# Half of neighbourhood attention's output projection, worked in halves inside latent attention

## Chip, cores, metric

One core of one Trainium2 chip. The metric is device microseconds (us) of one execution of the whole program. Before the change three runs took 2887.43, 2887.59 and 2888.29 us; the median is 2887.59 us.

## What is computed

The reference is one step of a two-layer trunk on 128 context tokens and 512 latent tokens of width 1024, 640 in all. Only the mixer of the first layer matters here. It runs two kinds of attention on the same input, 8 heads each, and projects both outputs together:

```python
def _even_mixer_latent(h, k_ctx, v_ctx, ckv_ctx, kr_ctx, w_in, q_norm, kv_norm, w_uq, w_ukv, rpb, w_out):
    qa, ka, va, qb, ckv, kr = _even_project(h, w_in, q_norm, kv_norm, w_uq)
    oa = _neighbourhood_attention(qa, ka, va, k_ctx, v_ctx, rpb)
    ...
    kb_lat, vb_lat = _mla_keys(ckv, _axial_rope(kr), w_ukv)
    kb_ctx, vb_ctx = _mla_keys(ckv_ctx, kr_ctx[:, :, None, :], w_ukv)
    ...
    ob = _blocked_attention(qb, kb, vb, (MLA_NOPE_DIM + MLA_ROPE_DIM) ** -0.5)
    return jnp.concatenate([oa.reshape(B, L, NA_WIDTH), ob.reshape(B, L, MLA_OUT)], axis=-1) @ w_out

xs = xs + ms[:, :, 5] * ys
```

The context tokens go through the same mixer, with plain attention among their own 128 keys. Since `w_out` is linear, the kernel adds the part of the neighbourhood heads to `x` first and the part of the latent heads later.

## The kernel before

Activations lie with channels on partitions and 640 tokens as columns. Weights arrive in blocks of 1024 columns: SP loads a block into one of 4 `raw` buffers, ScalarE (ACT) rounds it to the high part, VectorE (DVE) subtracts to get the low part; these two are the `split` of a block (L915 on ACT, L1541 on DVE), and the results lie in a ring of 4 `w2` slots. A slot is free when TensorE (PE) has used the block four before it (`wt_free`, the function `done`). A product is three matmuls (high x high, high x low, low x high) for each 128 channels and each half of the tokens, 320 columns at a time.

The mixer runs in this order on PE, in the engine's own program; blocks are counted from `n0`:

1. Neighbourhood attention (units of one head and 128 queries). Its output stays in `g2`.
2. `out_proj` (L2875, called on L2942): 8 output tiles of 128 channels from `g2`, two in each of the blocks `n0+18` to `n0+21`; a tile is 4 channel groups x 3 products x 2 halves = 24 matmuls. DVE adds each tile to `x` (`add_by_rows`, L1677 and L1679).
3. Block `n0+22`: values for latent attention (`tok_tiles`, L2714), copied to `va` by ACT. Blocks `n0+23` to `n0+26`: queries and keys (`ch_tile`, L2400), copied to `qb` and `kb` by ACT (L1348, L1357), rotated on DVE.
4. `latent_attention` (L2832): 32 units, 8 for each pair of heads. In unit `l` PE issues the scores of unit `l+2` (L2729, L2730), in some units the values of a pair of earlier units (L2807), and the 5 transposes of unit `l` (L2764). Around it DVE takes the maximum (L2122), ACT the exponential (L1255), DVE divides by the sum (L2129, L2130), and ACT copies the transposed weights to `pt` (L1264). The context tokens of a pair of heads run beside this: scores in unit 2 of 8 (L2772), transposes in unit 5, values in unit 7, in bank 7 of PSUM.
5. `last_out_proj`: 8 output tiles from the latent heads' output, which ACT and DVE have put in `g2` over the neighbourhood output; then norm and FFN.

The scores of unit `l+2` wait until the exponential of unit `l` has been taken, since there are two score buffers:

```python
            def score_mm(g):
                h, b = UNITS[g]
                pe.wait_ge(s_exp, g - 1)
```

Of the kernel before, what the change touches and what calls it, by code (L numbers as in the profile page):

```python
# [71 lines left out]
EM_PAIR = [0, 1, 3, 2, 0] + [(e - 4) % 3 for e in range(5, 14)]  # L72
V_BANK = [2, 3, 4, 5, 7]
# [177 lines left out]
def build(nc, a):  # L251
# [3 lines left out]
    with ctx:  # L255
# [140 lines left out]
        va = place("va", 6 * NLAT, at=h_at + (3 * 2 * T + 4 * (PAST + T)) * 4).rearrange("p (t c) -> p t c", t=6)  # L396
        pt_ctx = place("pt_ctx", 2 * P, at=h_at + (3 * 2 * T + 4 * (PAST + T) + 6 * NLAT) * 4)
# [94 lines left out]
        cx_mm, cx_neg, cx_exp, cx_p = sem("cx_mm"), sem("cx_neg"), sem("cx_exp"), sem("cx_p")  # L492
        cx_t, cx_ev, cx_pv, cx_low = sem("cx_t"), sem("cx_ev"), sem("cx_pv"), sem("cx_low")
# [140 lines left out]
        def pt_cols(g):  # L634

            return slice(g % 4 * P, (g % 4 + 1) * P)

# [270 lines left out]
        def _(act):  # L908
# [349 lines left out]
            def pt_evac(g, na):  # L1258
                h, b = UNITS[g]
                act.wait_ge(t_mm, g + 1)  # L1260
                if g >= 4:
                    act.wait_ge(pv_mm, NU if NU <= g < NU + 4 else g - 3)
                n = 1 if b == 0 else 3 if na else 5
                act.activation(pt[:, 0:n, pt_cols(g)],  # L1264
                               turned(g)[:, 0:n * P].rearrange("p (k q) -> p k q", k=n), ACT.Copy).then_inc(t_ev, 1)

            def ctx_exp(p):
                act.wait_ge(cx_neg, p + 1)
                if p:
                    act.wait_ge(cx_t, p)  # L1270
                for v in range(2):
                    c = 4 + 2 * (p % 2) + v
                    ins = act.activation(sb3[:, v * P:(v + 1) * P], ps[:, 7, (1 + v) * P:(2 + v) * P], ACT.Exp,
# [3 lines left out]
            def ctx_evac(p):  # L1277
                act.wait_ge(cx_t, p + 1)
                if p:
                    act.wait_ge(cx_pv, p)  # L1280
                act.activation(pt_ctx, ps[:, 7, P:3 * P], ACT.Copy).then_inc(cx_ev, 1)

            def o_lat(p, cols=slice(0, NLAT), src=ps[:, 6, :]):
                act.activation(lat_of(g2[:, p, 0, :])[:, cols], src[:, cols], ACT.Copy).then_inc(o_hi, 1)
# [41 lines left out]
            for m in range(4):  # L1326
                split(n0 + 18 + m + LEAD, (n0 + 18 + m + LEAD) % RING)
# [7 lines left out]
            split(n0 + 22 + LEAD, (n0 + 22 + LEAD) % RING)  # L1335
            for t in range(6):
                if t < 5:
                    act.wait_ge(vb_mm, t + 1)
                else:
                    act.wait_ge(wt_free, done(n0 + 22))  # L1340
                act.activation(va[:, t, :], ps[:, 2 + t, :], ACT.Copy).then_inc(vb_ev, 1)

            for p in range(4):
                n = n0 + 23 + p
                split(n + LEAD, (n + LEAD) % RING)
# [7 lines left out]
                for hh in range(2):  # L1353
                    if p == 3 and hh:
# [4 lines left out]
                                   ).then_inc(mk_ev, 1)  # L1359
            for l in range(2, NL):  # L1360
# [4 lines left out]
                if i == 3:  # L1365
                    ctx_exp(p)
                if i == 6:
                    ctx_evac(p)
                if i == 0:
                    if p == 1:  # L1370
                        act.wait_ge(wt_free, done(n0 + 21))
                    act.wait_ge(cx_pv, p)
                    o_ctx(p - 1)
                if i == 1:
                    act.wait_ge(pv_mm, NU + l - 1)
                    o_lat(p - 1)
            act.wait_ge(cx_pv, 4)
            o_ctx(3)
            act.wait_ge(pv_mm, NU + NL - 2)
            o_lat(3, slice(0, 3 * P))  # L1380
            pt_evac(NU + NL - 1, False)
            act.wait_ge(pv_mm, NU + NL)
            o_lat(3, slice(3 * P, NLAT), last_out)
            for j in range(4):
                n = n0 + 27 + j
                if j < 3:
                    split(n + LEAD, (n + LEAD) % RING)
# [139 lines left out]
        def _(dve):  # L1527
# [451 lines left out]
            def last_projection(nn, n0, out_at, g, xb, l, s):  # L1979

                norm_scale(l, s)
                for j in range(4):
                    n = out_at + j
                    if j < 3:
                        split(n + LEAD)
# [147 lines left out]
            def ctx_scores(p):  # L2133
                dve.wait_ge(cx_mm, p + 1)
                dve.tensor_reduce(negmax[:, cx_cols(p)], ps[:, 7, P:3 * P].rearrange("p (v k) -> p v k", v=2), AX.X,
                                  ALU.max, negate=True).then_inc(cx_neg, 1)

            def ctx_normalise(p):
# [3 lines left out]
                both = sb3[:, 0:2 * P].rearrange("p (v k) -> p v k", v=2)  # L2142
# [3 lines left out]
            def o_lat(p, cols=slice(0, NLAT), src=ps[:, 6, :]):  # L2146
                return dve.tensor_tensor(lat_of(g2[:, p, 1, :])[:, cols], src[:, cols],
                                         lat_of(g2[:, p, 0, :])[:, cols].bitcast(fp32), ALU.subtract)

            def o_ctx(p):  # L2150
                return dve.tensor_tensor(ctx_of(g2[:, p, 1, :]), ps[:, 7, 0:P],
                                         ctx_of(g2[:, p, 0, :]).bitcast(fp32), ALU.subtract)

# [36 lines left out]
            for j in range(4):  # L2190
# [4 lines left out]
            split(n0 + 22 + LEAD)  # L2195
# [8 lines left out]
            for p in range(4):  # L2204
                split(n0 + 23 + p + LEAD)
# [13 lines left out]
            for l in range(NL):  # L2219
                p, i = divmod(l, 8)  # L2220
                if 1 < l + 1 < NL:
                    scores(NU + l + 1, False)
                normalise(NU + l)
                if i == 2:
                    ctx_scores(p)
                if i == 4:
                    ctx_normalise(p)
                if i == 0 and p:
                    dve.wait_ge(o_hi, 8 + 2 * p - 1)
                    o_ctx(p - 1).then_inc(cx_low, 1)  # L2230
                if i == 1 and p:
                    dve.wait_ge(o_hi, 8 + 2 * p)
                    o_lat(p - 1).then_inc(o_lo, 1)
            dve.wait_ge(o_hi, 15)
            o_ctx(3)
            dve.wait_ge(o_hi, 16)
            o_lat(3, slice(0, 3 * P))
            dve.wait_ge(o_hi, 17)
            o_lat(3, slice(3 * P, NLAT), last_out).then_inc(o_lo, 1)
# [146 lines left out]
        def _(pe):  # L2386
# [366 lines left out]
            def weight_mm(g, na):  # L2753

                h, b = UNITS[g]
                pe.wait_ge(s_p, g + 1)
                if na and g >= 2:
                    pe.wait_ge(t_ev, g - 1)
                elif not na:
                    pe.wait_ge(t_ev, g - 1 if g >= NU + NL - 2 else g)  # L2760
# [580 lines left out]
```

## Time and profile before

| | us |
|---|---|
| median of the runs | 2887.59 |
| span of the profiled execution, first to last instruction | 2885.2 |
| median less that span | 2.4 |
| PE busy in the span | 2841.8 (98%) |
| DVE busy | 2112.8 (73%) |
| ACT busy | 1190.9 (41%) |
| output projection of neighbourhood attention and maps of latent attention (672.54 to 742.10 us from the span's start) | 69.56 |
| units of latent attention (742.10 to 822.57) | 80.47 |

The page of the profile gives one span and no own time for the profiled execution apart from it; what lies around the span is the 2.4 us between it and the median. "Busy" on PE counts from the first to the modelled end of each matmul, so a busy share says that matmuls follow each other closely, not that the array is full. The granted TensorE clock is 1.00 in both stretches, the higher of its two levels.

### The profile page before, as it was taken

Reading aid. Unit: us, or ns where it says so; the run is one execution under the profiler, and the core shown is the slowest. Engines: PE = TensorE matmul, PEld = TensorE weight load, DVE = VectorE, ACT = ScalarE, POOL = GpSimd, SP = SyncE. Lnnn points to the kernel's source line nnn. Section 1 sums busy time; section 2 is a strip of 40 time slices with the busy share of each in tenths; the row PEclk is TensorE's granted clock in tenths of the full one; section 3 lists DMA queues with packets and bytes.
Section 4 is the critical chain, followed back from the end, with each engine's and each line's share of the span. In section 5 each row is a group of like instructions: output and inputs, shape, how many; then the busy total and the mean of one; then the engine's idle time right before and its main releaser. Section 6 shows DMA issues by size and latency. Waiting matters only on the chain. (4 is left out here: it accounts for less than half of the span.)

```text
span 2885.2 us, 46747 instructions
## 1 busy us (share of the span) xinstructions
PE 2841.8 (98%) x18154; PEld 2658.3 (92%) x18154; DVE 2112.8 (73%) x4053; ACT 1190.9 (41%) x2212; POOL 347.7 (12%) x436
## 2 busy tenths in 40 slices
PE   8999999999999999999999999999999999999998
PEld 5999999978789999999999998798887988999998
DVE  5898987766768989778878775755747467866856
ACT  5433535254666334356334354223233144533433
POOL 1000003120031000021000022202112033000001
PEclk9999999999999999999999999999999999999999
DMA  7544343521014433424433222324223231422221
GB/s 258 147 150 132 107 127 119 180 74 47 23 46 131 152 119 105 130 79 116 130 100 103 92 96 94 111 94 125 68 87 116 81 132 37 105 78 88 76 86 66
DMA packets 94238, 303.52 MB, mean 105 GB/s; under 512 B 10753, under 2 KB 21281, under 8 KB 93121
## 3 DMA queue, kind: packets, MB, share of 16 engines
q1 hardware_dynamic: 67328, 223.03, 23.8%
q0 software_dynamic: 21296, 63.58, 8.0%
q10 hardware_dynamic: 5392, 13.92, 1.3%
q8 instruction: 144, 2.36, 0.3%
q14 instruction: 78, 0.63, 0.1%
HBM read 285.14 MB, written 7.49 MB: 101 GB/s over the span
## 5 line engine op out<-in xcount | busy, mean ns | idle before, releaser
L2566 PE MATMUL ps<-g,w 128*128 128x320 f32 x4224 | 624.8, 308 | 0.0
L2566 PEld LDWEIGHTS ps<-g,w 128*128 128x128 f32 x4224 | 620.6, 187 | 0.8
L2533 PE MATMUL ps<-h,w 128*128 128x320 f32 x3744 | 578.3, 309 | 8.4 <-ACT swu L1022 4.6
L2533 PEld LDWEIGHTS ps<-h,w 128*128 128x128 f32 x3744 | 556.0, 188 | 10.3 <-ACT swu L1022 5.7
L2533 PE MATMUL ps<-e,w 128*128 128x320 f32 x2808 | 437.3, 309 | 0.1
L2533 PEld LDWEIGHTS ps<-e,w 128*128 128x128 f32 x2808 | 418.2, 188 | 0.4 <-DMA e<-tsum 0.4
L1541 DVE TENSOR_TENSOR w<-raw,w 128x1024 fp32r<-128x1024 f32 (+1 forms) x243 | 277.5, 1146 | 160.9 <-ACT w L915 144.7
L2714 PE MATMUL ps<-w,h 128*128 128x512 f32 x1596 | 367.4, 391 | 0.1
L2714 PEld LDWEIGHTS ps<-w,h 128*128 128x128 f32 x1596 | 298.1, 188 | 62.7 <-ACT rg L1486 1.0
L928 ACT ACTIVATE w<-w2s 128x512 fp32r<-128x512 f32 x312 | 194.1, 631 | 275.2 <-DVE w2s L1693 84.2
L915 ACT ACTIVATE w<-raw 128x1024 fp32r<-128x1024 f32 x123 | 128.9, 1061 | 264.2 <-PE ps L2400 130.9
L1720 DVE TENSOR_TENSOR w<-w2s,w 128x512 fp32r<-128x512 f32 x312 | 209.6, 684 | 3.6 <-ACT w L928 2.4
L2400 PE MATMUL ps<-h,w 128*128 128x320 f32 (+1 forms) x1344 | 204.2, 312 | 0.0
L2400 PEld LDWEIGHTS ps<-h,w 128*128 128x128 f32 x1344 | 199.0, 188 | 1.7 <-issue 1.4
L1670 DVE SCALAR_TENSOR_TENSOR x<-ps,gate,x 128x128 f32<-128x128 f32 x216 | 108.3, 545 | 125.7 <-PE ps L2566 113.2
L922 ACT ACTIVATE w<-raw 128x768 fp32r<-128x768 f32 (+1 forms) x120 | 106.0, 886 | 220.9 <-PE ps L2566 189.0
L933 ACT ACTIVATE w<-raw 128x512 fp32r<-128x512 f32 x234 | 145.0, 624 | 70.4 <-PE ps L2566 70.1
L781 POOL DMA_DIRECT2D cond<-in_ada x80 | 43.0, 538 | 920.8 <-DVE acol L1556 914.9
L733 POOL TENSOR_TENSOR tmp_q<-tmp_q 128x320 f32<-128x320 f32 (+1 forms) x72 | 79.1, 1099 | 594.9 <-ACT tmp_q L962 585.9
L2400 PE MATMUL ps<-g,w 128*128 128x320 f32 x888 | 131.4, 309 | 0.0
L2400 PEld LDWEIGHTS ps<-g,w 128*128 128x128 f32 x888 | 130.4, 188 | 0.3 <-issue 0.3
L1556 DVE CUSTOM_DVE_ANT_0 unused<-cond,crow 128x512 f32<-128x512 f32 x160 | 110.1, 688 | 9.8 <-DMA cond<-in_ada 5.3
(305 smaller groups left out, 3672.4 us busy)
## 6 DMA issues: line engine op xcount, KB each, us to landing
raw<-in_ws SPq DMA_DIRECT2D x303, 512.0 KB, 3.7
cond<-in_ada POOLq DMA_DIRECT2D x80, 512.0 KB, 3.9
raw<-in_ws SPq DMA_DIRECT2D x96, 384.0 KB, 3.1
raw<-in_ada SPq DMA_DIRECT2D x32, 512.0 KB, 3.6
cond_em<-in_ada POOLq DMA_DIRECT2D x16, 512.0 KB, 3.9
e<-tsum POOLq DMA_DIRECT2D x12, 640.0 KB, 6.3
ada<-in_ada SPq DMA_DIRECT2D x5, 1024.0 KB, 17.9
rst<-in_state ACTq DMA_DIRECT2D x4, 1024.0 KB, 4.8
```

Of the source, the lines that this page charges most:

```text
L915: act.activation(w2[:, slot_of(n), 0, :], raw_of("w", n), ACT.Copy).then_inc(wt_hi, 1)
L922: act.activation(w2[:, slot_of(n), 0, 0:cols], raw_of("w", n)[:, 0:cols], ACT.Copy).then_inc(wt_hi, 1)
L928: act.activation(left(q, f, m, 0), left_value(q, f, m), ACT.Copy).then_inc(left_hi, 1)
L933: act.activation(left(q, f, m, 0), quarter(b, half), ACT.Copy).then_inc(left_hi if m == 0 else wt_hi, 1)
L1541: dve.tensor_tensor(w2[:, slot, 1, 0:cols], raw_of("w", n)[:, 0:cols], w2[:, slot, 0, 0:cols].bitcast(fp32), ALU.subtract).then_inc(wt_lo, 1)
L1556: dve.tensor_tensor_reduce(at if row else spare, at, rows[:, row, c0:c1], 1.0, 0.0, ALU.mult, ALU.add, acol[:, k, to:to + 1]).then_inc(ada ...
L1670: ins = dve.scalar_tensor_tensor(part(xn[:, m, :]), part(pair(pr)), g[:, m, st:st + 1], part(xn[:, m, :]), ALU.mult, ALU.add)
L1720: dve.tensor_tensor(lo, left_value(q, f, m) if m else quarter(n, 0), hi, ALU.subtract).then_inc(left_lo, 1)
L2400: mm = pe.matmul(pair_half(pr, half, width), w2[:, slot, wi, at:at + cols], rhs(k, ri)[:, half * width:(half + 1) * width], start=(k == 0 ...
L2533: mm = pe.matmul(ps[:, 4 * s + bank, 0:HT], w2[:, at // 2, wi, c:c + P], rhs(k, ri), start=start and k + wi + ri == 0, stop=(k == 3 and wi ...
L2566: mm = pe.matmul(pair_half(pr, half), w2[:, slot_of(n), wi, c:c + P], half_of(g2[:, k, ri, :], half), start=k + wi + ri == 0, stop=(k == n ...
L2714: mm = pe.matmul(ps[:, bank_of(t), :], ones_tile(src(k, ri), t), w2[:, slot_of(n), wi, kk * 512:(kk + 1) * 512], start=(k == 0 and ri == 0 ...
```

## The change

Four of the eight output tiles of neighbourhood attention (tiles 4 to 7) leave step 2. They are worked in halves inside latent attention: a half tile is 12 matmuls, three to a unit (six in unit 1, none in unit 0), all into bank 7 of PSUM, and DVE adds each half to `x` after its fourth group. The blocks of these tiles move behind the maps in the stream of weights (`n0+25` and `n0+26`; the values' block becomes `n0+20`), so the splits of the blocks after them come at other places: `n0+24` before the maps, one at the end of each of the four rounds of maps, and `n0+29` in unit 17. The context tokens' work in latent attention moves from bank 7 into the free columns of the transposes' bank 5 and to other units: scores in unit 0 of 8, transposes in unit 4, values in unit 5; ACT first copies the scores to `sbc` and takes the exponential from there. Since `g2` is still read, the latent heads' output goes to `m2`, which lies over `h2`.

The core of the diff:

```diff
+NA_OUT_FIRST = 2
+MLA_SLOTS = [0, 2] + [1] * 30
+MLA_HALVES = 2 * (KD - 2 * NA_OUT_FIRST)
+MLA_AT = {next(l for l in range(len(MLA_SLOTS)) if sum(MLA_SLOTS[:l + 1]) >= 4 * (d + 1)): d for d in range(MLA_HALVES)}
+MLA_SPLITS = {17: 29}
...
+        mla_ctx = ps[:, 5, P:3 * P]
...
+                if not na:
+                    mla_ctx_out(*divmod(g - NU, 8))
                 act.activation(pt[:, 0:n, pt_cols(g)],
...
+            def mla_ctx_out(p, i):
+
+                if i == 0:
+                    act.activation(sbc, mla_ctx, ACT.Copy).then_inc(cx_raw, 1)
+                if i == 4:
+                    act.activation(pt_ctx, mla_ctx, ACT.Copy)
+                if i == 5:
+                    if p:
+                        act.wait_ge(cx_low, p)
+                    act.activation(ctx_of(m2[:, p, 0, :]), mla_ctx[:, 0:P], ACT.Copy)
+                    act.activation(mctx, mla_ctx[:, 0:P], ACT.Copy).then_inc(o_hi, 1)
...
-                split(n + LEAD, (n + LEAD) % RING)
...
+                split(n + RING)
             for l in range(2, NL):
...
+                if l in MLA_SPLITS:
+                    split(n0 + MLA_SPLITS[l])
...
+            def add_na_half(d):
+
+                m, h = divmod(d + 4 * NA_OUT_FIRST, 2)
+                g = mod[:, 5, m, :]
+                if h and m % 2:
+                    dve.wait_ge(wt_free, done(na_out_block(m // 2)))
+                else:
+                    dve.wait_ge(na_half, d - d // 4 + 1)
...
+                if l - 1 in MLA_AT:
+                    add_na_half(MLA_AT[l - 1])
                 normalise(NU + l)
...
+                if l == 1:
+                    split(V_UP + RING + 4)
...
+            def na_out_steps(l):
+
+                for i in range(sum(MLA_SLOTS[:l]), sum(MLA_SLOTS[:l + 1])):
+                    d, k = divmod(i, 4)
+                    m, h = divmod(d + 4 * NA_OUT_FIRST, 2)
+                    n = na_out_block(m // 2)
+                    if d == 0 and k == 0:
+                        pe.wait_ge(mk_ev, MLH)
+                    if k == 0 and h == 0 and m % 2 == 0:
+                        have(n)
+                    if k == 0 and h:
+                        pe.wait_ge(na_add, d // 2 + 1)
+                    elif k == 0 and d:
+                        pe.wait_ge(x_upd, EM_X + m)
+                    at = m % 2 * 4 * P + k * P
+                    for wi, ri in ((0, 0), (0, 1), (1, 0)):
+                        mm = pe.matmul(ps[:, 7, 0:HT], w2[:, slot_of(n), wi, at:at + P], half_of(g2[:, k, ri, :], h),
+                                       start=(k == 0 and wi == 0 and ri == 0), stop=(k == 3 and wi == 1))
+                    if k == 3:
+                        mm.then_inc(wt_free if h and m % 2 else na_half, 1)
...
+                    na_out_steps(l)
                     if l != NL - 2:
                         weight_mm(g, False)
...
+            out_proj(n0 + 18, EM_X, 4, 0, blocks=NA_OUT_FIRST)
```

How the instructions now stand, at the three places that matter. PE, between the last values of neighbourhood attention (`va_ctx`) and the maps; before:

```order
L2807 MATMUL ps<-pt 64x128 x2
L2807 MATMUL ps<-pt,va_ctx 64x128 x2
L2400 MATMUL ps<-g_89,w_55 128x320 x192
L2714 MATMUL ps<-w_55,h_50 128x512 x36
L2400 MATMUL ps<-h_50,w_55 128x320 x36
```

and now:

```order
L2861 MATMUL ps<-pt 64x128 x2
L2861 MATMUL ps<-pt,va_ctx 64x128 x2
L2442 MATMUL ps<-g_89,w_55 128x320 x96
L2756 MATMUL ps<-w_55,h_50 128x512 x36
L2442 MATMUL ps<-h_50,w_55 128x320 x36
```

Half of the projection's 192 matmuls are gone from here; nothing else on PE moves at this place.

PE, in latent attention (transposes `ident,sb`, scores `kb,qb`, values `pt,va`); before, from the transposes of unit 8 to those of unit 10:

```order
L2764 MATMUL ps<-ident,sb_120 128x128 x5
L2729 MATMUL ps<-kb_128,qb 128x512
L2730 MATMUL ps<-kb_128,qb 128x128
L2764 MATMUL ps<-ident,sb_120 128x128 x5
L2729 MATMUL ps<-kb_127,qb 128x512
L2730 MATMUL ps<-kb_127,qb 128x128
L2772 MATMUL ps<-kb_127,qb 128x128
L2772 MATMUL ps<-kb_128,qb 128x128
L2764 MATMUL ps<-ident,sb_124 128x128 x5
```

and now, from the transposes of unit 6 to the context scores in unit 8:

```order
L2807 MATMUL ps<-ident,sb_120 128x128 x5
L2771 MATMUL ps<-kb_128,qb 128x512
L2772 MATMUL ps<-kb_128,qb 128x128
L2840 MATMUL ps<-g_89,w_55 128x320 x3
L2807 MATMUL ps<-ident,sb_124 128x128 x5
L2771 MATMUL ps<-kb_127,qb 128x512
L2772 MATMUL ps<-kb_127,qb 128x128
L2861 MATMUL ps<-pt,va 64x128 x10
L2840 MATMUL ps<-g_89,w_55 128x320 x3
L2815 MATMUL ps<-kb_127,qb 128x128
```

Three matmuls of the projection (L2840) stand ahead of the transposes of every unit; the context scores (L2772 before, L2815 now) come two units earlier.

ACT, around unit 17 (exponentials write `sb`, copies of the transposed weights write `pt`, the latent output goes to `g_89` before, to `h_50` now); before:

```order
L1264 ACTIVATE pt<-ps 128x5x128
L1287 ACTIVATE g_89<-ps 128x128
L1255 ACTIVATE sb_120,rsum<-ps,negmax 128x640
L1264 ACTIVATE pt<-ps 128x5x128
L1284 ACTIVATE g_89<-ps 128x512
L1255 ACTIVATE sb_120,rsum<-ps,negmax 128x640
```

and now:

```order
L1271 ACTIVATE sb_120,rsum<-ps,negmax 128x640
L1288 ACTIVATE sbc<-ps 128x256
L1282 ACTIVATE pt<-ps 128x5x128
L1306 ACTIVATE h_50<-ps 128x512
L931 ACTIVATE w_55<-raw 128x1024
L1271 ACTIVATE sb_120,rsum<-ps,negmax 128x640
```

The copy of the context scores (L1288) and, in this unit alone, a split (L931) now stand ahead of the next exponential.

## Rows read from the trace of the kernel before

**Rows 1.** Busy time by engine in two stretches (us, busy, instructions; granted clock)

```profile
core 0: us, PE busy (x) PEld busy (x) DVE busy (x) ACT busy (x) POOL busy (x), PEclk, DMA share, GB/s
672.54:742.10 69.56, 69.56 (x434) 66.31 (x432) 48.95 (x79) 24.89 (x34) 0.00 (x0) 1.00 0.23 71
742.10:822.57 80.47, 77.10 (x636) 56.16 (x636) 50.94 (x113) 54.10 (x124) 0.56 (x1) 1.00 0.04 14
```

**Rows 2.** Timeline of PE, projection and values' block: start, us, line, tiles, [idle before]

```profile
672.54 28.43 PE L2400 MATMUL ps<-g,w 128*128 128x320 f32 x192
700.81 8.32 PE L2714 MATMUL ps<-w,h 128*128 128x512 f32 x36
708.97 24.91 PE L2400 MATMUL ps<-h,w 128*128 128x320 f32 x162
```

**Rows 3.** Page, costliest groups: weight loads of the projection's matmuls

```profile
L2400 PEld LDWEIGHTS ps<-g,w 128*128 128x128 f32 x888 | 130.4, 188 | 0.3 <-issue 0.3
```

**Rows 4.** Timeline of PE: a run of map matmuls between two scores

```profile
733.73 1.02 PE L2729 MATMUL ps<-kb,qb 96*128 96x512 f32 x2
...
734.72 2.89 PE L2400 MATMUL ps<-h,w 128*128 128x320 f32 x18
737.59 1.10 PE L2729 MATMUL ps<-kb,qb 96*128 96x512 f32 x2
```

**Rows 5.** Timeline of PE, retention layer: transposes amid a run of 512-column matmuls

```profile
1790.22 0.82 PE L3012 MATMUL ps<-ident,rk 128*128 128x128 f32 x6
1790.80 7.08 PE L2714 MATMUL ps<-w,h 128*128 128x512 f32 x30
1797.71 0.60 PE L3012 MATMUL ps<-ident,rk 128*128 128x128 f32 x4
```

**Rows 6.** Timeline of PE in latent attention: start, one unit, the waits

```profile
742.59 0.74 PE L2764 MATMUL ps<-ident,sb 128*128 128x128 f32 x5 [0.49 <-DVE sb L2130]
...
744.24 0.71 PE L2764 MATMUL ps<-ident,sb 128*128 128x128 f32 x5
...
762.81 0.76 PE L2764 MATMUL ps<-ident,sb 128*128 128x128 f32 x5
763.41 1.02 PE L2729 MATMUL ps<-kb,qb 96*128 96x512 f32 x2
...
764.49 0.71 PE L2764 MATMUL ps<-ident,sb 128*128 128x128 f32 x5
765.63 1.12 PE L2729 MATMUL ps<-kb,qb 96*128 96x512 f32 x2 [0.43 <-ACT sb L1255]
...
817.62 0.76 PE L2764 MATMUL ps<-ident,sb 128*128 128x128 f32 x5 [0.81 <-DVE sb L2130]
...
821.33 1.31 PE L2807 MATMUL ps<-pt,va 128*64 128x128 f32 x20 [0.79 <-ACT pt L1264]
```

**Rows 7.** Timeline of ACT: a split, key copies, context copy, unit 9

```profile
732.83 1.04 ACT L915 ACTIVATE w<-raw 128x1024 fp32r<-128x1024 f32 x1
...
744.87 0.81 ACT L1357 ACTIVATE kb<-ps 64x768 f32<-64x768 f32 x1
...
756.03 0.38 ACT L1281 ACTIVATE pt_ctx<-ps 128x256 f32<-128x256 f32 x1
...
763.61 0.70 ACT L1264 ACTIVATE pt<-ps 128x640 f32<-128x640 f32 x1 [1.37 <-PE ps L2764]
764.21 0.59 ACT L1284 ACTIVATE g<-ps 128x512 fp32r<-128x512 f32 x1
764.69 0.80 ACT L1255 ACTIVATE sb<-ps,negmax 128x640 f32<-128x640 f32 x1
```

**Rows 8.** Timeline of DVE: a split, then one unit's maximum and division

```profile
733.91 1.23 DVE L1541 TENSOR_TENSOR w<-raw,w 128x1024 fp32r<-128x1024 f32 x1 [1.37 <-ACT w L915]
...
744.45 0.82 DVE L2122 TENSOR_REDUCE negmax<-ps 128x1 f32<-128x640 f32 x1 [0.72 <-PE ps L2730]
...
745.38 0.55 DVE L2130 TENSOR_SCALAR sb<-sb,rinv 128x640 f32<-128x640 f32 x1
```

**Rows 9.** Instructions of DVE's add of a projection tile's latent columns (ns min/median/max)

```profile
L1679 DVE SCALAR_TENSOR_TENSOR x<-ps,mod,x x8: 1171/1232/1259, 680.2 to 702.8; 128x512 f32<-128x512 f32 x8
```

More of the change, by code:

```diff
@@ L1325, in _ @@
             o_ctx(3)
-            for m in range(4):
-                split(n0 + 18 + m + LEAD, (n0 + 18 + m + LEAD) % RING)
+            for m in range(2 + NA_OUT_FIRST):
+                split(n0 + 18 + m + LEAD)
             act.wait_ge(em_ld4, 32)
@@ L1983, in last_projection @@
                     n = out_at + j
-                    if j < 3:
+                    if j < 3 and (j or nn != 2):
                         split(n + LEAD)
@@ L2189, in _ @@
             dve.wait_ge(ada_ev, 6)
-            for j in range(4):
+            for j in range(NA_OUT_FIRST):
                 split(n0 + 18 + j + LEAD)
@@ L2194, in _ @@
                     add_by_rows(m, (m + 1) % 4, mod[:, 5], EM_X + m + 1)
-            split(n0 + 22 + LEAD)
+            for j in range(2):
+                split(n0 + 18 + NA_OUT_FIRST + j + LEAD)
             dve.wait_ge(em_ld4, 32)
@@ L2204, in _ @@
             for p in range(4):
-                split(n0 + 23 + p + LEAD)
+                split(V_UP + RING + p)
                 for hh in range(2):
@@ L2765, in weight_mm, with mla_ctx_step @@
                 mm.then_inc(t_mm, 1)
-            def ctx_score_mm(p):
-                if p:
-                    pe.wait_ge(cx_low, p)
+            def mla_ctx_step(p, i):
                 for v in range(2):
-                    mm = pe.matmul(ps[:, 7, (1 + v) * P:(2 + v) * P], ctx_of(qb[0:NOPE + ROPE, 2 * p + v, :]),
-                                   ctx_of(kb[2 * p + v][0:NOPE + ROPE, PAST:]), start=True, stop=True)
-                mm.then_inc(cx_mm, 1)
-            def ctx_weight_mm(p):
-                pe.wait_ge(cx_p, p + 1)
-                for v in range(2):
-                    mm = pe.transpose(ps[:, 7, (1 + v) * P:(2 + v) * P], sb3[:, v * P:(v + 1) * P], ident)
-                mm.then_inc(cx_t, 1)
@@ L2783, in ctx_value_mm @@
-            def ctx_value_mm(p):
-                pe.wait_ge(cx_ev, p + 1)
-                for v in range(2):
-                    mm = pe.matmul(ps[64 * v:64 * v + 64, 7, 0:P], va[:, 5, (2 * p + v) * 64:(2 * p + v) * 64 + 64],
-                                   pt_ctx[:, v * P:(v + 1) * P], start=True, stop=True)
-                mm.then_inc(cx_pv, 1)
+                    part = mla_ctx[:, v * P:(v + 1) * P]
+                    if i == 0:
+                        pe.matmul(part, ctx_of(qb[0:NOPE + ROPE, 2 * p + v, :]),
+                                  ctx_of(kb[2 * p + v][0:NOPE + ROPE, PAST:]), start=True, stop=True)
@@ new lines, in mla_ctx_step @@
+                    if i == 4:
+                        pe.wait_ge(cx_p, p + 1)
+                        pe.transpose(part, sbc[:, v * P:(v + 1) * P], ident)
+                    if i == 5:
+                        pe.matmul(mla_ctx[64 * v:64 * v + 64, 0:P], va[:, 5, (2 * p + v) * 64:(2 * p + v) * 64 + 64],
+                                  pt_ctx[:, v * P:(v + 1) * P], start=True, stop=True)
+            def na_out_steps(l):
[17 more added lines that the diff above has]
+                        mm.then_inc(wt_free if h and m % 2 else na_half, 1)
@@ L2873, in _, with out_proj @@
             attend_pairs()
-            def out_proj(n, xb, lag, lo, pairs=None, before_last_pair=None):
-                for j in range(4):
+            def out_proj(n, xb, lag, lo, pairs=None, before_last_pair=None, blocks=4):
+                for j in range(blocks):
                     have(n + j)
@@ L3193, in stream_blocks, with na_output @@
     wo = w["mix_w_out"][0]
-    output(wo[:na])
+    na_out = tiles(wo[:na])
+    def na_output(j0, j1):
+        for j in range(j0, j1):
+            put(na_out[:, :, 2 * j * P:(2 * j + 1) * P], na_out[:, :, (2 * j + 1) * P:(2 * j + 2) * P])
+    na_output(0, NA_OUT_FIRST)
     ukv = w["mla_w_ukv"][0].reshape(KVR, MLH, NOPE + VD)
```

140 lines of the change are left out of this document (73 added, 67 removed).

## The prediction

> **What bounds the kernel now.** I read the busy time of the two stretches first, then PE's timeline through them, then what ACT and DVE do where PE waits. PE has no idle time at all from the projection through the maps (69.56 of 69.56 us) and little in latent attention (77.10 of 80.47, so 3.37 idle), at a granted clock of 1.00, the 2.4 GHz level [rows 1]. DVE and ACT are busy for 50.94 and 54.10 us of the latter stretch: there is room on them, but their order decides who waits. The reader should see one thing: the change moves PE work from a place where PE never waits to a place where PE waits 3.37 us. That is about the most that filling waits can win, 0.12% of the time. The waits are the 0.49 at the first transposes, 0.43 in each of three pairs of heads (at 765.63 and twice more, 20.5 us apart), 0.81 and 0.79 at the end [rows 6]; they add up to 3.38. A difference under 0.2% (5.8 us) is what a measurement of this kernel can hardly tell from none.
>
> **Work that leaves the projection.** 192 matmuls start to start take 700.81 - 672.54 = 28.27 us, 0.147 us each [rows 2]. 96 of them go: -14.1 us. PE stays dense behind them: the values' block needs only banks whose tiles have been added, and DVE has four adds fewer to do (1.23 us each for the latent columns alone [rows 9]). I cost the earlier place of the values' block and the reordered splits ahead of the maps at nothing: the adds that go away cover them, and the maps' own splits stand where they stood on ACT, right behind the key copies of a round. If that cover is gone, one split (1.04 on ACT, 1.23 on DVE [rows 7, 8]) shows. SP loads the same blocks in another order, with no wait on PE in this stretch to show that one is late [rows 1]; POOL's queue is not moved past.
>
> **Work that enters latent attention.** The same 96 matmuls: +14.1 us. What counts is the rest: seams and waits.
>
> **Seams.** They come in 30 runs (six in unit 1, three in each of units 2 to 29, six in 30 and 31 together), each between fp32 matmuls of another kind. The trace shows no run of three there, so I bound a seam. Scores, 18 map matmuls, scores takes 737.59 - 733.73 = 3.86 us; the scores' own 1.08 (763.41 to 764.49 [rows 6]) and 18 x 0.147 leave 0.13 for the seam [rows 4]. Six transposes and 30 matmuls of 512 columns take 1797.71 - 1790.22 = 7.49; at 0.227 a matmul ((708.97 - 700.81) / 36 [rows 2]) and 0.108 a transpose (scores are two passes of 640 columns in 1.08, so one pass of 128 takes a tenth) they should take 7.45: a seam of 0.04 [rows 5]. From below I take 0, as a run can hide its first weight load behind what runs; from above a weight load of 0.188 shown on both sides, 0.38 [rows 3]. I take 0.08, between the two measured seams, since the neighbours here are transposes on one side in all 30 and scores on the other in some: 30 x 0.08 = +2.4 (bounds 0 and +11.3).
>
> Against the 0.08 stands a rule. In the uniform projection a matmul with a 188 ns load of its own takes 147 ns, so loads overlap there [rows 2, 3]. The Trainium skill (TensorE: Matmul & The Clock Gate, in "What overlaps and what doesn't") says that a weight load overlaps a running matmul only when their row groups differ. All these matmuls use the full height of the array, so by that rule every load would show; the trace disagrees in the uniform stream, and at a seam it has only the two cases above. By the rule the seams would be 11.3 us, not 2.4.
>
> **Waits.** A group of three is worth 3 x 0.147 + 0.08 = 0.52 us of cover in each unit.
> - First transposes: the context scores now stand ahead of them; the 0.49 is filled.
> - Unit 1: the first group waits for the last key copy on ACT, since bank 7 holds that map. Before, it ended at 744.87 + 0.81 = 745.68; the copy of the context scores (0.38, priced by the same shape to `pt_ctx`) now comes ahead of it: 746.06 [rows 7]. PE is there at 744.24 [rows 6]: 1.82 of waiting.
> - Unit 2: behind that copy ACT splits block `n0+28` (1.04) and DVE waits to split it (1.23) in front of its next maximum; then 0.93 to the division and 0.55: 746.06 + 1.04 + 1.23 + 1.48 = 749.81 [rows 7, 8]. PE, with six matmuls (0.96), transposes (0.60), scores (1.08) and a group (0.52), is at the transposes of unit 2 at 749.22: 0.6 of waiting.
> - The three waits of 0.43: unit 9's run on ACT is copy of weights, copy of output, exponential (763.61, 764.21, 764.69), and the next scores start when that ends [rows 6, 7]. The new context copy adds 0.38 to it, the group gives PE 0.52 more to do: 0.43 + 0.38 - 0.52 = 0.29 each, 0.87.
> - Unit 17: a split (1.04) stands in the same run on ACT, in front of the exponential of unit 18. PE waits there already, so all of it shows: 1.04, once. Its DVE half (1.23) follows the division of unit 18, which is late already; I cost it at nothing.
> - The end: 0.81 - 0.52 = 0.29; the 0.79 stays, since the last transposes have nothing behind them but their copy.
>
> Sum after: 1.82 + 0.6 + 0.87 + 1.04 + 0.29 + 0.79 = 5.41 us, against 3.38: +2.0. The bounds: all waits but the last filled, -2.6; each estimate doubled where it is new (1.82, 0.6, 1.04), +5.5. DVE's eight half adds cost under 1.23 us each, the price of 512 columns [rows 9], and come in units with values, where PE has transposes (0.60), scores (1.08) and values (1.24, 821.33 to the stretch's end [rows 1, 6]) to do, 2.9 us, before it asks for bank 7 again; I cost them at nothing, and at a late handover's price (third rival) if that cover is gone.
>
> **Sum.** -14.1 + 14.1 + 2.4 + 2.0 = +4.4 us. On the span of 2885.2 that is 2889.6, and with the 2.4 around it, as the median stands to the span, **2892.0 us**: no change that counts.
>
> **The rivals.**
> - *Waits filled, seams free.* For: PE's list has a group in every unit, ACT and DVE have a third of the stretch idle, and both new waits at the start rest on my shifting of rows. Then the 3.38 falls to the last 0.79: 2885.0. To be faster by more than 5.8 us it would need gains that no wait here offers. Chance 0.22.
> - *Seams show their weight loads.* The slower side, one mechanism: at each of 30 seams PE can't load the next weights while a matmul of another kind runs, 0.38 each. It decides from 0.13 a seam up (30 x 0.13 + 2.0 = 5.9). For: the score seam is already 0.13; against: the transposes' seam of 0.04 and the overlap in the uniform run [rows 2 to 5]. 2887.6 + 11.3 + 2.0 = 2900.9. Chance 0.11. Beside it stands the rule of the Trainium skill (TensorE: Matmul & The Clock Gate, "What overlaps and what doesn't"), which gives the same price.
> - *Bank 7 is handed over late.* One bank holds all half tiles, so a group that begins a half waits for DVE's add, which stands behind a maximum (0.82) in DVE's order. If DVE runs a unit late, 7 handovers cost about 0.8 each (that maximum): 2892.0 + 5.6 = 2897.6. Against: the 2.9 us of PE work in between. Chance 0.07.
>
> **How the numbers follow.** The forecast has 0.60; its seams (0.04 to 0.13 each) and waits (0 to +4) spread it over about 2889 to 2895, and a sixth of it lies above 2893.4, the bound of slower. Slower: 0.10 + 0.11 + 0.07 = 0.28. Faster: 0.03, out of the first rival. The same: 0.69. The range of 2884.5 to 2897.5 holds the forecast, most of the first rival and half of the third; what is left out is the seams' rival and the tails, about 0.2.
>
> **What would show it.** In the changed profile the projection's row should have 96 matmuls in 14.1 us and the maps no wait. The units should take 80.5 + 14.1 + 4.4 = 99 us. Unit 1's first group should carry a wait on ACT's key copy of about 1.8 us, unit 2's transposes one on DVE of about 0.6, and the scores of unit 20 one on ACT's exponential of over 1 us. A pair of heads without the split should take 20.5 + 24 x 0.147 + 8 x 0.08 - 0.14 = 24.5 us. I am wrong if those eight units take under 23.8 (seams free) or over 26 (loads shown), if PE waits at bank 7's handovers, or if the stretch behind latent attention changes, where I expect nothing.

## The result and the profile after

| | before | changed |
|---|---|---|
| median of 20 runs each, us | 2887.55 | 2890.89 |
| lowest to highest | 2885.03 to 2891.64 | 2889.26 to 2894.89 |
| span of the profiled execution | 2885.2 | 2890.9 |

The ratio is 1.0012, with a 95% interval from 1.0007 to 1.0018: 3.3 us more, 0.12%. That is slower, but under the 0.2% which the prediction took as the bound of "no change". 2892.0 was forecast.

The profile of one execution has to be read with care here, since the two spans differ by 5.7 us. I compare the stretch from the projection's first matmul to the first matmul of the last projection, which holds all that the change touches on PE. It takes 822.57 - 672.54 = 150.03 us before [rows 1, 2] and 828.41 - 675.26 = 153.15 now: **+3.12 us**, which agrees with the medians. Behind it nothing changed: 2062.6 us before, 2062.5 now. Ahead of it the profiled execution lost 2.7 us. Most of that lies where the granted clock of this one execution was lower than that of the other: 0.95 against 0.98 between 25 and 100 us, 0.76 and 0.50 against 1.00 from 184 to 188 us, and 0.50 to 0.69 against 1.00 from 628 to 636 us. This differs from execution to execution and is no effect of the change.

About 0.3 us ahead of the stretch do belong to the change. From the scores at 624.99 us to the projection, through neighbourhood attention, the kernel before takes 672.54 - 624.99 = 47.55 us. The eight kernels of the experiments below take 47.85 to 47.88 between the same two instructions, all at a granted clock of 1.00; their transposes wait a little longer (0.98 against 0.89 us for the first of them). The change also swaps the two waits ahead of these transposes (in `weight_mm`, a part of the diff that is not shown); whether that is the reason was not tested. With these 0.3 the 3.12 become 3.4, where the medians have 3.3.

The busy times of the two parts of that stretch in the changed kernel (columns as in [rows 1]):

```profile
675.26:731.05 55.79, 55.79 (x343) 52.68 (x341) 42.07 (x71) 24.12 (x35) 0.00 (x0) 1.00 0.24 78
731.05:828.41 97.36, 92.23 (x730) 70.14 (x728) 58.01 (x125) 57.32 (x133) 0.56 (x1) 1.00 0.07 23
```

Projection and maps still have no idle time (55.79 of 55.79), the units 97.36 - 92.23 = 5.13, and the clock is 1.00. PE's timeline of the changed kernel, which answers to [rows 2, 6], in the order of the program (projection; units 1 and 2; a unit without values; the scores that wait for the split; the last units):

```profile
675.26 14.35 PE L2442 MATMUL ps<-g,w 128*128 128x320 f32 x96
689.45 8.35 PE L2756 MATMUL ps<-w,h 128*128 128x512 f32 x36
...
731.05 0.77 PE L2807 MATMUL ps<-ident,sb 128*128 128x128 f32 x5
...
734.49 1.16 PE L2840 MATMUL ps<-g,w 128*128 128x320 f32 x6 [1.59 <-ACT kb L1378]
...
738.18 0.74 PE L2807 MATMUL ps<-ident,sb 128*128 128x128 f32 x5 [0.47 <-DVE sb L2145]
...
752.21 1.02 PE L2771 MATMUL ps<-kb,qb 96*128 96x512 f32 x2
753.07 0.38 PE L2772 MATMUL ps<-kb,qb 96*128 96x128 f32 x2
753.21 0.69 PE L2840 MATMUL ps<-g,w 128*128 128x320 f32 x3
753.74 0.71 PE L2807 MATMUL ps<-ident,sb 128*128 128x128 f32 x5
754.28 1.02 PE L2771 MATMUL ps<-kb,qb 96*128 96x512 f32 x2
...
760.73 1.12 PE L2771 MATMUL ps<-kb,qb 96*128 96x512 f32 x2 [0.26 <-ACT sb L1271]
...
785.87 1.12 PE L2771 MATMUL ps<-kb,qb 96*128 96x512 f32 x2 [1.20 <-ACT sb L1271]
...
810.08 1.12 PE L2771 MATMUL ps<-kb,qb 96*128 96x512 f32 x2 [0.27 <-ACT sb L1271]
...
822.47 0.74 PE L2807 MATMUL ps<-ident,sb 128*128 128x128 f32 x5 [0.16 <-DVE sb L2145]
823.44 1.31 PE L2861 MATMUL ps<-pt,va 128*64 128x128 f32 x20 [0.23 <-ACT pt L1282]
...
827.17 1.31 PE L2861 MATMUL ps<-pt,va 128*64 128x128 f32 x20 [0.79 <-ACT pt L1282]
828.41 0.86 PE L2442 MATMUL ps<-h,w 128*128 128x320 f32 x4
```

These are all of PE's recorded waits in the stretch; they add up to 4.97 us, where those of before made 3.38 [rows 6]. So of the 3.12 us, 4.97 - 3.38 = 1.59 are waits, and the other 1.53 lie between the instructions. What stands ahead of the two longest waits is on ACT's timeline of the changed kernel, where the second run answers to that of unit 9 before [rows 7]:

```profile
733.63 0.81 ACT L1378 ACTIVATE kb<-ps 64x768 f32<-64x768 f32 x1
734.34 1.04 ACT L931 ACTIVATE w<-raw 128x1024 fp32r<-128x1024 f32 x1
...
782.92 0.70 ACT L1282 ACTIVATE pt<-ps 128x640 f32<-128x640 f32 x1
783.50 0.61 ACT L1306 ACTIVATE h<-ps 128x512 fp32r<-128x512 f32 x1
783.98 1.07 ACT L931 ACTIVATE w<-raw 128x1024 fp32r<-128x1024 f32 x1
784.92 0.81 ACT L1271 ACTIVATE sb<-ps,negmax 128x640 f32<-128x640 f32 x1
```

The key copy ends at 733.63 + 0.81 = 734.44, and bank 7's first matmul starts at 734.49. The split stands at 783.98 ahead of the exponential, and the scores start at 785.87, behind its end.

### The profile page after: what moved, and what is told of

It is laid out like the page before. It is cut to its first block and busy times, and to the rows that moved or that the text cites. A ratio compares the mean times of both kernels' runs of the same rounds, so it can differ in the third digit from the quotient of the medians.

```text
span 2890.9 us, 46745 instructions
## 1 busy us (share of the span) xinstructions
PE 2848.8 (99%) x18154; PEld 2664.0 (92%) x18154; DVE 2112.5 (73%) x4057; ACT 1192.4 (41%) x2220; POOL 347.5 (12%) x436
## 5 line engine op out<-in xcount | busy, mean ns | idle before, releaser
L2608 PE MATMUL ps<-g,w 128*128 128x320 f32 x4224 | 624.9, 308 | 0.0
L2608 PEld LDWEIGHTS ps<-g,w 128*128 128x128 f32 x4224 | 620.6, 188 | 0.8
L2575 PEld LDWEIGHTS ps<-h,w 128*128 128x128 f32 x3744 | 557.5, 188 | 8.7 <-ACT swu L1038 5.2
L931 ACT ACTIVATE w<-raw 128x1024 fp32r<-128x1024 f32 x123 | 129.0, 1061 | 257.7 <-PE ps L2442 124.5
L2442 PE MATMUL ps<-h,w 128*128 128x320 f32 (+1 forms) x1416 | 215.0, 312 | 0.0
L2442 PEld LDWEIGHTS ps<-h,w 128*128 128x128 f32 x1416 | 209.6, 188 | 1.8 <-issue 1.6
L2442 PE MATMUL ps<-g,w 128*128 128x320 f32 x720 | 106.5, 309 | 0.0
L1730 DVE TENSOR_TENSOR w<-raw,w 128x512 fp32r<-128x512 f32 x156 | 106.4, 684 | 0.0
```

Source lines behind the costliest of these rows:

```text
L931: act.activation(w2[:, slot_of(n), 0, :], raw_of("w", n), ACT.Copy).then_inc(wt_hi, 1)
L1730: dve.tensor_tensor(lo, quarter(n + m - 5, 1), hi, ALU.subtract).then_inc(wt_lo, 1)
L2442: mm = pe.matmul(pair_half(pr, half, width), w2[:, slot, wi, at:at + cols], rhs(k, ri)[:, half * width:(half + 1) * width], start=(k == 0 ...
L2575: mm = pe.matmul(ps[:, 4 * s + bank, 0:HT], w2[:, at // 2, wi, c:c + P], rhs(k, ri), start=start and k + wi + ri == 0, stop=(k == 3 and wi ...
L2608: mm = pe.matmul(pair_half(pr, half), w2[:, slot_of(n), wi, c:c + P], half_of(g2[:, k, ri, :], half), start=k + wi + ri == 0, stop=(k == n ...
```

## The experiments

Two theories were set against each other. *Waits*: what the change costs lies in waits that the new order of ACT and DVE makes, and a switch between kinds of matmul is nearly free. *Seams*: each switch costs 0.2 to 0.38 us, a weight load's time. All runs are judged by the same stretch. Each kernel has one profile; in one profile the same unit repeats within 0.02 us from one pair of heads to the next, so differences from about 0.2 us up are read. "Rest" in the table is the stretch less its recorded waits. In some of the kernels PE's lines stand one lower and DVE's one higher than in the changed kernel. The single times of e1_split20 to e4_ctx_alone are from a chip on which the kernel before took 2889.28 us in its one run; the others are from one on which its median was 2887.45.

| kernel | stretch | waits | rest | groups' runs | median us (runs) |
|---|---|---|---|---|---|
| before | 150.03 | 3.38 | 146.65 | 0 | 2887.55 (20) |
| changed | 153.15 | 4.97 | 148.18 | 30 | 2890.89 (20) |
| e1_split20 | 152.23 | 4.04 | 148.19 | 30 | 2888.27 (1) |
| e2_start2 | 155.21 | 5.22 | 149.99 | 29 | 2891.70 (1) |
| e3_start2_splits | 150.74 | 2.29 | 148.45 | 29 | 2887.91 (1) |
| e4_ctx_alone | 158.40 | 6.23 | 152.17 | 0 | 2893.84 (1) |
| e5_pairs_plain | 150.67 | 3.74 | 146.93 | 16 | 2888.41 (1) |
| e9_seams_twice | 149.85 | 1.28 | 148.57 | 55 | 2890.12 (1) |
| e7_all | 150.21 | 1.83 | 148.38 | 29 | 2886.59 (11) |
| e8_pairs_all | 148.19 | 1.25 | 146.94 | 16 | 2885.07 (11) |

Single times scatter by more than the differences in the stretch (the one of e9_seams_twice is among the higher ones though its stretch is shorter than before's), so the stretch decides there.

**The split of block n0+29 in unit 20.**

```diff
-MLA_SPLITS = {17: 29}
+MLA_SPLITS = {20: 29}
```

> The split of block n0+29 stands in unit 20 (a unit with values) in place of unit 17; nothing else differs from the changed kernel. Measured on the stretch from the projection's first matmul to the first matmul of the last projection: 150.03 us before, 153.15 with the change. Theory of waits (the +3.1 us are PE's waits on ACT's and DVE's order, seams are small): the wait of 1.20 us ahead of the scores of unit 20 falls to the 0.26 of its two sisters, no new wait appears behind unit 20, and the stretch is 152.2. Rival, theory of seams (the loss is the 30 changes between kinds of matmul): PE gets the time back as waits elsewhere, the stretch stays at 153.1.

The stretch became 152.23, 0.92 shorter. The scores that waited 1.20 now wait 0.26 as in the other pairs (PE's timeline of this run):

```profile
782.99 1.12 PE L2771 MATMUL ps<-kb,qb 96*128 96x512 f32 x2 [0.26 <-ACT sb L1271]
```

On ACT's timeline of this run the exponential now follows the copy of the output at once, and the split stands three units later, where its exponential isn't waited for:

```profile
781.56 0.61 ACT L1306 ACTIVATE h<-ps 128x512 fp32r<-128x512 f32 x1
782.04 0.81 ACT L1271 ACTIVATE sb<-ps,negmax 128x640 f32<-128x640 f32 x1
...
789.53 1.05 ACT L931 ACTIVATE w<-raw 128x1024 fp32r<-128x1024 f32 x1
```

So the split's place costs 0.92 us of the change's 3.12, as the waits' theory had it; the rest (148.19) is unchanged.

**The first groups in units 2 and 3.** This takes the wait on the key copy away.

```diff
-MLA_SLOTS = [0, 2] + [1] * 30
+MLA_SLOTS = [0, 0, 2, 2] + [1] * 28
```

> The projection's groups begin in unit 2 (six matmuls each in units 2 and 3) in place of unit 1; nothing else differs from the changed kernel. If the wait for the key copy (1.59 us in unit 1) is a cost of its own, it goes and the stretch falls from 153.15 to about 151.6. My theory: the start is set by one chain, key copy, split of n0+28 on ACT, the same split on DVE, maximum, division, which lets the transposes of unit 2 begin about 7.1 us after those of unit 0 whatever PE does before; so the wait only moves to the transposes of unit 2 (0.47 before, over 2 now), one group fewer is done by then, and the stretch is 153.4 to 153.7.

The expectation had 151.6 if the wait was a cost of its own, and 153.4 to 153.7 if one chain sets the start. The stretch took 155.21, above both and 2.06 more than the changed kernel. The wait on the key copy is gone, but in its place the transposes of unit 2 wait 2.30 for DVE (PE's timeline of this run, and DVE's):

```profile
736.54 0.74 PE L2807 MATMUL ps<-ident,sb 128*128 128x128 f32 x5 [2.30 <-DVE sb L2145]
737.11 1.42 PE L2771 MATMUL ps<-kb,qb 96*128 96x512 f32 x2
...
738.88 2.34 PE L2861 MATMUL ps<-pt,va 128*64 128x128 f32 x20
```

```profile
733.77 1.23 DVE L1556 TENSOR_TENSOR w<-raw,w 128x1024 fp32r<-128x1024 f32 x1 [2.70 <-ACT w L931]
734.91 0.82 DVE L2137 TENSOR_REDUCE negmax<-ps 128x1 f32<-128x640 f32 x1
```

These transposes start 736.54 - 729.40 = 7.14 us after those of unit 0, against 738.18 - 731.05 = 7.13 in the changed kernel: the chain key copy, split on ACT, split on DVE, division sets that moment, and moving the groups only moves the wait. This much was expected. The other part was not: the granted clock fell after the wait (busy time by stretch in this run, columns as in [rows 1], the clock is the third number from the end):

```profile
736.50:738.00 1.50, 1.46 (x7) 1.06 (x8) 1.43 (x5) 0.84 (x4) 0.00 (x0) 0.87 0.83 317
738.00:740.00 2.00, 2.00 (x13) 1.46 (x13) 1.14 (x2) 0.79 (x3) 0.00 (x0) 0.50 0.01 4
740.00:742.00 2.00, 2.00 (x19) 1.73 (x17) 0.00 (x0) 0.00 (x0) 0.00 (x0) 0.74 0.00 0
742.00:744.00 2.00, 2.00 (x14) 1.39 (x14) 1.48 (x5) 1.12 (x2) 0.00 (x0) 1.00 0.00 0
```

At 0.50, the 1.2 GHz level, the values that take 1.24 in the changed kernel (739.93 to 741.17) take 741.15 - 738.88 = 2.27. The rest of this run stands 149.99 - 148.18 = 1.81 above the changed kernel's, and this is where it lies. Without it the stretch would be 153.40, the lower end of what the chain was to give. Whether the clock falls behind such a wait differs between executions (last section), so the 1.81 belong to this execution.

**The same, with both splits moved.** The split of `n0+28` leaves the start for unit 4, that of `n0+29` goes to unit 20.

```diff
-MLA_SLOTS = [0, 2] + [1] * 30
+MLA_SLOTS = [0, 0, 2, 2] + [1] * 28
-MLA_SPLITS = {17: 29}
+MLA_SPLITS = {4: 28, 20: 29}
...
-                split(n + RING)
+                if p < 3:
+                    split(n + RING)
...
-                if l == 1:
-                    split(V_UP + RING + 4)
```

> As the run that begins in unit 2, and the split of n0+28 leaves the start: it is done in unit 4, that of n0+29 in unit 20. Theory of waits: the chain at the start loses 2.3 us of splits, the transposes of unit 2 begin about 4.7 us after those of unit 0 with two groups done, the wait of 1.20 falls to 0.26, and the stretch is 150.0 to 150.6, level with the kernel before. Theory of seams: 30 groups less one are still there, the stretch stays above 152.5.

150.74, 0.14 above the waits' range and far below the seams': 0.71 above before, with all 96 matmuls in the units. On PE's timeline of this run the start has 0.32 of waiting left, where the changed kernel has 1.59 + 0.47:

```profile
734.51 1.12 PE L2770 MATMUL ps<-kb,qb 96*128 96x512 f32 x2 [0.32 <-ACT sb L1271]
```

The clock stays at 1.00 there. So three edits of the order take back 2.41 of the 3.12 us, with 29 runs of the groups in place of 30.

**The moves of the context stream and of the splits, without the groups.** All eight tiles stay in the projection; the context work of latent attention stands as in the changed kernel, and so do the splits of the maps: the last of them comes behind the last key copy (745.81 us on ACT), where the last of the kernel before stands a round earlier (732.83 [rows 7]).

```diff
-NA_OUT_FIRST = 2
-MLA_SLOTS = [0, 2] + [1] * 30
+NA_OUT_FIRST = 4
+MLA_SLOTS = [0] * 32
-MLA_SPLITS = {17: 29}
+MLA_SPLITS = {}
...
-                if 0 < j < 3:
+                if 1 < j < 3:
...
-            add_na_half(MLA_HALVES - 1)
```

> The other half of the change alone: all eight tiles stay in the projection as before, and only the context stream's move (bank 5, earlier units, its copies ahead of the transposes' copies on ACT) and the moved splits ahead of unit 2 are in; no split in unit 17, no groups. No seams of the projection are left. Theory of waits: without the groups as cover the start shows the whole chain of splits (3 to 4 us at the transposes of unit 2) and the three waits behind the copies in units 8, 16 and 24 grow from 0.43 to about 0.8; the stretch is 153.5 to 154.5, worse than the whole change. Theory of seams: without seams the stretch is back at 150 to 151.

Both were too low: 158.40, 8.37 above before. The waits grew by 6.23 - 3.38 = 2.85, above all at the transposes of unit 2, which have no groups ahead of them to cover the chain of splits; the three waits behind the copies grew only from 0.43 to 0.49, where 0.8 was expected (PE's timeline of this run, and the clock behind that wait):

```profile
749.65 1.02 PE L2806 MATMUL ps<-ident,sb 128*128 128x128 f32 x5 [3.18 <-DVE sb L2145]
750.46 1.92 PE L2770 MATMUL ps<-kb,qb 96*128 96x512 f32 x2
```

```profile
749.60:751.00 1.40, 1.35 (x6) 1.18 (x7) 1.33 (x4) 0.46 (x3) 0.00 (x0) 0.63 0.89 328
751.00:753.00 2.00, 2.00 (x6) 0.94 (x6) 0.58 (x2) 1.19 (x3) 0.00 (x0) 0.50 0.05 14
753.00:754.30 1.30, 1.30 (x21) 1.13 (x19) 1.26 (x3) 0.00 (x0) 0.00 (x0) 0.85 0.00 0
```

Weighted by these shares, the stretch from 749.60 to 754.30 lost 1.40 x 0.37 + 2.00 x 0.50 + 1.30 x 0.15 = 1.7 us to the clock. The remainder, 8.37 - 2.85 - 1.7 = 3.8, is spread: the second pair of heads takes 789.92 - 768.26 = 21.66 us here (from one unit 0's transposes to the next) and 20.5 before, 1.2 more with only 0.06 of it in recorded waits. It is in gaps between starts that are 0.1 to 0.25 longer and that the view doesn't mark as waits; what ends each of them was not taken apart. So what the change moves besides the groups is a loss by itself, the split at the start above all; how much of the 3.8 is the context stream's is not shown, since this run moves both. In the changed kernel the groups of three cover most of it: there a pair of heads takes 24.2 us, 3.7 more than before for 24 x 0.147 = 3.5 of matmuls. (Putting ACT's context copies behind its copy of the transposes, to take them out of that run, was not tried.)

**Groups in sixes, mainly in units without values.**

```diff
-MLA_SLOTS = [0, 2] + [1] * 30
+MLA_SLOTS = [0, 2, 2, 0, 0, 2, 0, 2] * 4
```

> Groups come as six matmuls in units 1 and 2 and then mainly in units without values: 16 runs of projection matmuls in latent attention in place of 30, with the splits left where they are. The units with context work that waited 0.26 us at the scores now have six matmuls in front of them. Theory of waits (seams nearly free, measured at 0.00 in units without values and about 0.05 in units with them): the stretch from the projection's first matmul to that of the last projection falls from 153.15 to about 150.9 us: 0.7 from seams, 0.5 from the two waits of 0.26, 0.44 from the split's 1.20, 0.16 to 0.4 at the start and end. Theory of seams (each shows 0.2 to 0.38): it falls by 14 x 0.2 to 0.38, 2.8 to 5.3, more, to 145 to 148.

150.67, near the 150.9 of the waits' theory, where that of seams had 145 to 148; the waits of 0.26 are gone, the split's fell to 0.77. The rest fell from 148.18 to 146.93, almost the 146.65 of before: in this arrangement 96 matmuls cost their own time in the units and only 0.28 more.

**Seams doubled.** As the version with both splits moved, but in units 4 to 29 two matmuls of a group stand ahead of the transposes and one behind them.

```diff
-                    na_out_steps(l)
+                    cut = 3 < l < NL - 2
+                    na_out_steps(l, (0, 2 if cut else 3))
                     if l != NL - 2:
                         weight_mm(g, False)
+                    if cut:
+                        na_out_steps(l, (2, 3))
```

> As the version with first groups in unit 2 and both splits moved (150.74 us for the stretch), but in units 4 to 29 each group of three is cut in two: two matmuls ahead of the transposes, one behind them. 26 seams more, no work more. Theory of waits: a cut costs 0 to 0.05 us as the existing seams do, 0 to 1.3 us in all, a stretch of 150.5 to 152.1. Theory of seams (0.38 each): +9.9, about 160.6. At the 0.08 each of the prediction it would be +2.1, 152.8.

149.85: 26 seams more, and 0.89 us *less*. PE's timeline of this run shows a unit of one pair of heads:

```profile
761.90 0.54 PE L2839 MATMUL ps<-g,w 128*128 128x320 f32 x2
762.28 0.71 PE L2806 MATMUL ps<-ident,sb 128*128 128x128 f32 x5
762.75 0.39 PE L2839 MATMUL ps<-g,w 128*128 128x320 f32 x1
762.98 1.08 PE L2770 MATMUL ps<-kb,qb 96*128 96x512 f32 x2
```

The transposes come 0.15 earlier and the matmul behind them fills the time in which PE waited for ACT: the three waits of 0.26 and the 0.24 at the end are gone, 1.01 in all. The rest moved from 148.45 to 148.57, so 26 seams cost 0.12 net, under 0.005 us each. Unmarked gaps that the extra seams filled can hide little: even if all by which e3_start2_splits stands above before's rest (148.45 - 146.65 = 1.80) had gone that way, a seam would be (0.12 + 1.80) / 26 = 0.07 us. This is the run that the seams' theory can't survive.

**All edits together.** As the version with both splits moved, and the last two groups between the last transposes and the last values. The first of the two versions keeps groups of three, the second has them in sixes.

```diff
-MLA_SLOTS = [0, 2] + [1] * 30
+MLA_SLOTS = [0, 0, 2, 2] + [1] * 26 + [0, 2]
...
-                    na_out_steps(l)
+                    if l < NL - 1:
+                        na_out_steps(l)
                     if l != NL - 2:
                         weight_mm(g, False)
+                    if l == NL - 1:
+                        na_out_steps(l)
```

> First groups in unit 2, the splits of blocks n0+28 and n0+29 in units 4 and 20, and the last two groups behind the last transposes, where PE waits 0.79 us for the copy to pt. Theory of waits: 150.74 less the 0.79 and 0.1 to 0.4 of other waits, a stretch of 149.6 to 149.9, level with 150.03 before the change; in time 2887.0 to 2887.6 us, the same as before. Theory of seams: 30 seams stay and the stretch stays above 152, 2889.5 us or more.

150.21, 0.3 above the range, and 2886.59 us: a ratio to before of 0.9996 (0.9987 to 1.0005), no difference. The 0.79 is filled, but the last transposes no longer have six matmuls (0.99 us in the changed kernel, 824.68 to 825.67) ahead of them and wait for DVE instead (PE's timeline of this run):

```profile
819.59 0.74 PE L2806 MATMUL ps<-ident,sb 128*128 128x128 f32 x5 [0.34 <-DVE sb L2146]
820.08 1.12 PE L2839 MATMUL ps<-g,w 128*128 128x320 f32 x6
```

In the second version the table is:

```diff
-MLA_SLOTS = [0, 0, 2, 2] + [1] * 26 + [0, 2]
+MLA_SLOTS = [0, 0, 2, 2, 0, 2, 0, 2] + [0, 2, 2, 0, 0, 2, 0, 2] * 3
```

> The same with the groups in sixes, mainly in units without values (15 runs of projection matmuls in place of 30), so that six matmuls also stand in front of the three waits of 0.26 us. Theory of waits: 0.7 from seams and 0.8 from the three waits less than the version with all three edits: a stretch of 148.3 to 148.8 us, 1.2 to 1.7 under the kernel before; in time 2885.8 to 2886.6 us. That is nearly all that filling waits can give, since 150.03 less its 3.38 of waits is 146.65. Theory of seams: 15 x 0.38 = 5.7 on top of 146.65, above 152.

(The 15 runs of the expectation are 16.) 148.19, just under the expected range, with 2885.07 us beside 2887.45 for before on the same chip: a ratio of 0.9989 (0.9980 to 0.9998), 2.4 us or 0.1% less, and so below both kernels; like the change's own, it is a difference under the bound of 0.2%, and the stretch, 1.84 shorter, carries it. All its recorded waits, on PE's timeline:

```profile
733.61 1.12 PE L2770 MATMUL ps<-kb,qb 96*128 96x512 f32 x2 [0.32 <-ACT sb L1271]
...
815.87 1.31 PE L2860 MATMUL ps<-pt,va 128*64 128x128 f32 x20 [0.59 <-ACT pt L1282]
817.52 0.74 PE L2806 MATMUL ps<-ident,sb 128*128 128x128 f32 x5 [0.34 <-DVE sb L2146]
```

1.25 us are left where before has 3.38. Little more is to be had in this stretch by filling waits.

## Why the prediction was right, and which term was off

The forecast was +4.4 us, the medians show +3.3 and the stretch +3.12, inside its range. Its waits came one by one as it named them, but for a small one. Its seams did not: the 1.53 us that stand where it had 2.4 are not the price of seams, so that this half of the sum came out near by luck.

- *Work that leaves the projection*: -14.1 predicted; 96 matmuls take 689.45 - 675.26 = 14.19 us and have no wait. The values' block in its new place and the reordered splits cost nothing, as taken.
- *Seams*: the mis-sized term. Predicted +2.4 (30 x 0.08). All that is not in recorded waits came to 1.53, and that is no price of a seam: 26 seams more cost 0.12, and the same 96 matmuls in 16 runs leave 0.28 or 0.29. What failed is that a group's seams were counted as added. The group's row is what I worked out: 753.21 to 753.74, 0.53, against 3 x 0.147 + 0.08 = 0.52. But the scores ahead of it take 753.21 - 752.21 = 1.00, where scores that transposes follow took 1.08, and transposes behind a group 0.54, where they took 0.60 behind values [rows 6]. The seam from scores to transposes was there already, and the group takes its place: 0.54 + 1.00 + 0.53 = 2.07 for the unit, 0.60 + 1.08 = 1.68 before, 0.39 for three matmuls that cost 0.44 elsewhere. What is left is uneven: beyond its matmuls and its marked waits a pair of heads takes 24.21 - 0.26 = 23.95 us, and 23.56 in e8_pairs_all. Of these 0.39, 0.17 each lie in the units 2 and 3 of the eight and 0.11 in unit 6, -0.06 in unit 7, and nothing in the others. Units 3 and 6 have a group behind values, but so has unit 4, at no cost; why just these was not taken apart, so that the cause of most of the 1.53 stays open; it goes when the groups come in sixes.
- *Waits*: +2.0 predicted, +1.59 measured. Unit 1's key copy 1.82 against 1.59: the copy came when predicted (3.44 us after the first transposes, 3.47 by the shifted rows), but the wait is counted from the modelled end of the scores (732.51 + 0.38), 1.84 behind the first transposes, where I had counted from the start at which transposes had followed, 1.65. Unit 2's split on DVE 0.6 against 0.47. The context copy: 0.29 against 0.26 and 0.27. Unit 17's split 0.29 + 1.04 = 1.33 against 1.20. The end 0.29 + 0.79 against 0.16 + 0.23 + 0.79, of which the 0.23 (the values before the last wait for their copy) was not named. e1_split20 and e3_start2_splits show that the splits make the waits that they were blamed for; e2_start2 shows that at the start the key copy and the split are one chain, so that its two waits can't be removed one at a time. A term that the sum doesn't have is the 0.3 us ahead of the projection.
- *The rivals.* Waits filled and seams free: the second half was nearer the truth than the forecast, the first failed through the places of the key copy and of two splits. With those moved, the last groups too, and the groups in sixes, its time is reached (e8_pairs_all at 2885.07, the rival's price 2885.0). Weight loads at each seam: e9_seams_twice would have had +9.9 and had -0.89, and what is left over in a unit of the changed kernel is 0.17 at most, not 0.38. The Trainium skill (TensorE: Matmul & The Clock Gate, "What overlaps and what doesn't") says that a weight load overlaps matmuls in flight only when their row groups differ; these runs don't agree with it. (Not all these matmuls use the full height of the array, as the prediction has it: the scores use 96 of the 128 partitions [rows 4].) Bank 7 handed over late: no group but the very first carries a recorded wait, so DVE's eight half adds were covered, as costed.
- *What would show it.* A pair of heads without the split: 810.08 - 785.87 = 24.21, predicted 24.5, between the bounds of 23.8 and 26. The units: 97.36 from the first transposes, 97.8 with the context scores ahead of them, predicted 99; the difference is 0.9 of seams and 0.4 of waits. Nothing behind latent attention: 2062.5 against 2062.6.

## What to carry to other kernels

Work moved from a place without waits into one with waits can win at most those waits, so read their sum first; then list what stands ahead of each waiting instruction on the other engines after the move, since a split of 1 us in the wrong unit gives the whole of it back. When a short run of matmuls is set between two others, price the seams as what is there after less what was there before: the run replaces a seam rather than adding two. And a wait on a chain of several steps only moves when one consumer is moved; move the step in the chain that isn't needed yet.

## What the runs showed of the chip that was not expected

A wait of 2.30 us on PE in e2_start2 and one of 3.18 us in e4_ctx_alone were each followed by a granted clock of 0.50, the lower level, over the 2 us from 738 and from 751 us on; by 742 and 754.3 us it was 1.00 again. In the changed kernel the waits of 1.59 and 0.47 left it at 1.00. By the excess of the rest, the first cost about 1.8 us on top of its own length, nearly as much as the wait itself.

The length of the wait alone doesn't settle it. One wait of 2.5 us, early in the program and outside the change, stands in all ten kernels. The same 24 matmuls follow it (PE's timeline of the kernel before, then of the changed kernel):

```profile
183.89 3.78 PE L2533 MATMUL ps<-h,w 128*128 128x320 f32 x24 [2.52 <-DVE swu L1821]
184.41 5.32 PE L2575 MATMUL ps<-h,w 128*128 128x320 f32 x24 [2.52 <-DVE swu L1836]
```

They take 3.78 or 3.79 us in four of the profiles, at a granted clock of 1.00, and 5.31 to 5.33 in the other six, where it falls to 0.50. So after a wait of this size in a dense stretch the clock may fall or not, and the wait can cost more than the trace's bracket says.

In both experiments a burst of DMA stands where the clock falls (0.83 and 0.89 busy, in their rows above). The burst alone doesn't do it: in e3_start2_splits one of 0.89 came without a wait on PE, and the clock stayed at 1.00 (busy time by stretch, columns as in [rows 1]):

```profile
745.00:746.00 1.00, 1.00 (x5) 0.45 (x3) 0.05 (x1) 0.93 (x4) 0.00 (x0) 1.00 0.89 365
```
